# A projection that fills idle TensorE time, in one chain through all stages of a decoder step, and a recurrence prepared per unit five steps ahead

## The reference

```python
h = rmsnorm(x) @ w_in     # fq fk fv ff fz hq hf hi hz mq mz ga gb gm, 1024 -> 8712 columns
o_fox = softmax(q k^T * scale + cq - ck) v            # 8 heads x 64, causal, 2048 rows
S = exp(bl)[..., None] * S + (k * exp(bl - b))^T v    # 4 heads x 128, state 128 x 128
o_mem = softmax(q mk^T * scale) mv                    # 4 heads x 128, 256 tokens
y = x + (sigmoid(ga)*ya + sigmoid(gb)*yb + sigmoid(gm)*ym) @ w_o
```

## Time and profile before

| | us |
|---|---|
| three runs | 3645.16, 3646.96, 3648.72 |
| median | 3646.96 |
| the profiled execution | 3645.66 |
| its span, first to last instruction | 3644.1 |

### The profile page before, as it was taken

One profiled execution on the slowest core, in us unless ns is written; L12 is line 12 of the kernel. 1 busy time (PEld: TensorE's weight loads), 2 busy tenths in 40 slices (PEclk: granted clock), 3 DMA queues, 4 the chain that ended last, 5 costly groups with the idle time before them and its releaser, 6 DMA issues. The chain is left out here.

```text
span 3644.1 us, 38245 instructions
## 1 busy us (share of the span) xinstructions
PE 2951.2 (81%) x13930; PEld 2335.6 (64%) x13930; DVE 1490.2 (41%) x2774; ACT 954.3 (26%) x1806; POOL 581.9 (16%) x539
## 2 busy tenths in 40 slices
PE   4969999999239777868499999999922386799999
PEld 3847777887127565657377787778822232588887
DVE  3510001111345454553455555555556622544444
ACT  1201111111023232222244454444400110423222
POOL 2021111110252324140201002020035300000000
PEclk8979999999559898989799999999966698899999
DMA  3325422211446454534555545554366476533331
GB/s 133 104 63 160 144 67 70 70 67 51 162 152 199 150 169 144 186 121 155 168 151 148 157 130 151 150 157 138 100 211 203 129 220 193 189 114 115 120 120 47
DMA packets 304488, 499.36 MB, mean 137 GB/s; under 512 B 109028, under 2 KB 150535, under 8 KB 285607
## 3 DMA queue, kind: packets, MB, share of 16 engines
q1 hardware_dynamic: 298399, 479.43, 41.9%
q0 software_dynamic: 5904, 17.51, 1.6%
HBM read 386.18 MB, written 110.67 MB: 136 GB/s over the span
## 5 line engine op out<-in xcount | busy, mean ns | idle before, releaser
L2246 PE MATMUL hgfill_out<-hgfill_w_hi,hgfill_x 128*128 128x512 f32 x1024 | 360.4, 429 | 77.4 <-DMA hgfill_x<-x_tiles 50.9
L2246 PE MATMUL fill_out<-fill_w_hi,fill_x 128*128 128x512 f32 x1024 | 374.4, 418 | 0.0
L477 DVE TENSOR_TENSOR in_stage<-in_stage,in_out 128x512 f32<-128x512 f32 x64 | 44.0, 687 | 624.3 <-ACT in_stage L466 624.3
L2246 PEld LDWEIGHTS hgfill_out<-hgfill_w_hi,hgfill_x 128*128 128x128 f32 x1024 | 204.3, 205 | 128.2 <-issue 53.5
L823 DVE TENSOR_TENSOR fox_pt_lo<-fox_turned,fox_pt_hi 128x512 fp32r<-128x512 f32 (+1 forms) x320 | 194.9, 609 | 191.5 <-ACT fox_pt_hi L773 189.9
L773 ACT ACTIVATE fox_pt_hi<-fox_turned 128x512 fp32r<-128x512 f32 (+1 forms) x320 | 170.4, 533 | 361.2 <-PE fox_turned L728 360.6
L809 DVE CUSTOM_DVE_ANT_0 fox_probs<-fox_scores,fox_bias 128x512 f32<-128x512 f32 (+2 forms) x320 | 187.8, 609 | 108.3 <-PE fox_scores L717 66.9
L179 PE MATMUL in_out<-x_hi,in_whi 128*128 128x512 f32 x512 | 205.9, 402 | 19.8 <-POOL in_wlo L421 19.8
L466 ACT ACTIVATE in_stage<-in_out 128x512 f32<-128x512 f32 x112 | 67.0, 599 | 588.0 <-PE in_out L181 588.0
L2246 PE MATMUL hgfill_out<-hgfill_w_lo,hgfill_x 128*128 128x512 f32 x512 | 217.5, 425 | 0.0
L2246 PE MATMUL fill_out<-fill_w_lo,fill_x 128*128 128x512 f32 x512 | 212.2, 414 | 0.0
(11 more groups left out here) (374 smaller groups left out, 6141.4 us busy)
## 6 DMA issues: line engine op xcount, KB each, us to landing
hgfill_x<-x_tiles SPq DMA_DIRECT2D x64, 1024.0 KB, 5.5
fill_x<-x_tiles SPq DMA_DIRECT2D x64, 1024.0 KB, 5.4
paged_slot<-in_cache_fox_k_dram SPq DMA_DIRECT2D x128, 256.0 KB, 3.0
paged_slot<-in_cache_fox_v_dram SPq DMA_DIRECT2D x128, 256.0 KB, 3.0
mf_gate<-plain SPq DMA_DIRECT2D x96, 256.0 KB
turned<-in_stage SPq DMA_DIRECT2D x64, 256.0 KB
plain<-fill_stage SPq DMA_DIRECT2D x64, 256.0 KB, 5.4
in_raw<-in_w_in_dram SPq DMA_DIRECT2D x56, 256.0 KB, 3.1
```

The lines of the kernel that those rows point to most:

```text
L477: dve.tensor_tensor(stage[u % STAGES][:], stage[u % STAGES][:], out[u % STAGES][:], ALU.mult).then_inc(taken, 1)
L2246: ins = pe.matmul(self.out[n % self.OUTS][:], x, w, start=(k == 0 and term == 0), stop=(ends and term == 2))
```

## The change

One Filler with all eight groups lives from the sample stages to the end of `attend_memory`, and each stage says how many of the 3200 matmuls it takes: 40 in `unpack_sample`, 190 in 16 slots of `attend_cache`, 170 in 10 slots of `recur_sample`, 1750 in 138 slots of the recurrence, 120 in 9 slots ahead of the first key step of `attend_prompt`, 80 in its 640 slots, and the 850 left in 66 slots of `attend_memory`. The loops of the sample stages are written out, since slots differ. `lower_bound` moves into `unpack_sample`. To leave two PSUM banks to the Filler, `attend_memory` has one bank of scores and one of turned probabilities where it had two of each. In the recurrence `prepare` comes after `early` and `late` of a step, five steps ahead of the unit's first chunk, five steps with no chunk go first, SP stores a finished piece two steps later and loads a unit three steps earlier. The Filler stores a unit when the next one ends.

```diff
 def recur_prompt(...):
+    PARTS, AHEAD = 4, 5
     def walk(prepare, early, late, post, extra):
-        for n, (blk, h, c) in enumerate(chunks):
-            if n == 0:
-                prepare(0)
-            if c == 0 and n // CH + 1 < len(units):
-                prepare(n // CH + 1)
-            early(n)
-            if n > 0:
+        for n in range(-AHEAD, len(chunks)):
+            if n >= 0:
+                early(n)
+            if n >= 1:
                 late(n - 1)
-            if blk > 0 and n % BLOCK in POST_AT:
-                post(blk - 1, POST_AT.index(n % BLOCK))
+            if n >= BLOCK and n % BLOCK in POST_AT:
+                post(n // BLOCK - 1, POST_AT.index(n % BLOCK))
+            u, at = divmod(n + AHEAD, CH)
+            if at == 0 and u < len(units):
+                for part in range(PARTS):
+                    prepare(u, part)
             extra(n)
...
 def attend_memory(...):
-        scores, turned, o_sum = psum("scores", 2), psum("turned", 2), psum("o_sum", 1)[0]
+        scores, turned, o_sum = (psum(n, 1)[0] for n in ("scores", "turned", "o_sum"))
+        fill.begin(fill.spread(matmuls, 2 * paged.GROUPS + 2))
...
             for u in range(NT + 2):
+                if u == 0:
+                    extra(0)
+                    extra(1)
...
                     elif u < NT:
                         values(n // paged.SLOTS, n % paged.SLOTS)
+                    if u < NT:
+                        extra(2 + u * PER + n % PER)
...
-                        if n >= 2:
-                            pe.wait_ge(exp_ready, n - 1)
+                        if n >= 1:
+                            pe.wait_ge(exp_ready, n)
...
 class Filler:
     def sync(self, sp, slot):
         for n in self.units_ending(self.until(slot), self.until(slot + 1)):
             g = self.group_of(self.first_unit, n)
             m = self.first_x[g] + n - self.first_unit[g]
             if not self.is_sample(n) and m + self.RING < self.first_x[-1]:
                 self.load_x(sp, m + self.RING)
-            self.store(sp, n)
+            if n >= 1:
+                self.store(sp, n - 1)
+            if n == self.units - 1:
+                self.store(sp, n)
...
+MATMULS = {"unpack": 40, "cache": 190, "sample": 170, "recur": 1750, "first": 120, "fox": 80}
```

More of the change, by code:

```diff
@@ L495, in attend_prompt @@
     quads = [(h, q) for h in range(FH) for q in range(QUADS)]
-    steps = [("set", 0)] + [("keys", 0, b) for b in range(QUADS)]
+    steps = [("fill", 0), ("set", 0)]
+    for b in range(QUADS):
+        steps += [("fill", 1 + b), ("keys", 0, b)]
     for i in range(4):
-        steps += [("score", 0, i, 0), ("exp", 0, i)]
+        steps += [("score", 0, i, 0), ("fill", 1 + QUADS + i), ("exp", 0, i)]
+    FILLS = 1 + QUADS + 4
     for n, (h, q) in enumerate(quads):
@@ L653, in _ @@
                     load_bias(0)
-                    fill.sync_start(sp)
                     for n in range(2):
@@ L1493, in _ @@
                 act.activation(sigmoid[:], part[0][:], ACT.Sigmoid).then_inc(sigmoid_ready, 1)
+                act.wait_ge(asked, 1)
+                act.activation(shifted[:], shifted[:], ACT.Exp).then_inc(exp_ready, 1)
+                fill.scalar(act, 0)
+            @block.tensor
+            def _(pe):
+                fill.tensor(pe, 0)
 class CacheAttention:
@@ L1795, in tensor_values, with attend_cache, walk, nothing @@
         m.then_inc(self.slot_free, 1)
-def attend_cache(nc, core, *arguments):
+def attend_cache(nc, core, fill, matmuls, *arguments):
     with ExitStack() as ctx:
         a = CacheAttention(nc, core, ctx, *arguments)
+        fill.begin(fill.spread(matmuls, 2 * a.GROUPS))
+        order = [(it, s) for it in range(a.ROUNDS) for s in range(a.SLOTS)]
+        def walk(keys, middle, values, extra):
+            for n, (it, s) in enumerate(order):
+                keys(it, s)
+                extra(n)
+            middle()
+            for n, (it, s) in enumerate(order):
+                values(it, s)
+                extra(a.GROUPS + n)
+        def nothing(*_):
+            return None
         with nc.Block() as block:
@@ L1885, in _ @@
                     sp.dma_start(primer[i:i + 1, :], core.ident[0:1, :]).then_inc(stored[i], 16)
-                with sp.Fori(0, B // 2) as it:
+                fill.sync(sp, 0)
+                for it in range(B // 2):
                     for i in range(2):
@@ L1912, in _ @@
                 m.then_inc(turned_ready, 1)
+                fill.tensor(pe, 0)
                 pe.wait_ge(step, 2 + 2 * HH)
-                with pe.Fori(0, B // 2) as it:
+                for it in range(B // 2):
                     for i in range(2):
@@ L1925, in _ @@
                 m.then_inc(back_ready, 1)
+                fill.tensor(pe, B + 1)
+            @block.gpsimd
+            def _(pool):
+                for slot in range(fill.slots):
+                    fill.gpsimd(pool, slot)
             @block.vector
@@ L1937, in _ @@
                 link.done[0] += 1
-                with dve.Fori(0, B // 2) as it:
+                for it in range(B // 2):
                     for i in range(2):
@@ L1965, in _ @@
                 act.sem_inc(taken, 2)
-                with act.Fori(0, B // 2) as it:
+                fill.scalar(act, 0)
+                for it in range(B // 2):
                     for i in range(2):
@@ L2203, in matmuls_of, with begin, spread, left @@
         return (len(group.tiles) - 1) * 3 * KT + KT * (5 if group.sample is not None else 3)
+    def begin(self, counts):
+        base = self.edges[-1]
+        self.edges = [base + sum(counts[:n]) for n in range(len(counts) + 1)]
+        self.slots = len(counts)
+        assert self.edges[-1] <= self.total
+    @staticmethod
+    def spread(matmuls, slots):
+        return [matmuls * (n + 1) // slots - matmuls * n // slots for n in range(slots)]
+    def left(self):
+        return self.total - self.edges[-1]
     def until(self, slot):
-        return self.total * min(slot, self.slots) // self.slots
+        return self.edges[slot]
     def group_of(self, counts, n):
```

384 lines of the change are left out of this document (201 added, 183 removed).

## The result

| | before | after |
|---|---|---|
| median us | 3647.24 (4 runs, 3645.16 to 3648.72) | 3860.43 (4 runs, 3850.31 to 3871.83) |
| the profiled execution | 3645.66 | 3871.83 |
| its span | 3644.1 | 3870.0 |

The changed kernel is slower: the ratio is 1.0586, with a 95% interval of 1.0556 to 1.0616. The forecast was 3790, with a range of 3560 to 3920.

What follows compares the result with a forecast made beforehand. PE was taken to bound the forget-gate attention and the memory value half, DVE and POOL the key half; samples +124, recurrence -56, forget-gate -264 and memory +340 gave +144 on 3645.7, 3790 us, range 3560 to 3920.

Steps and rivals of the forecast that it cites:

- Rival 2: Memory attention: the ring of pages doesn't run empty to any cost; stage grows by 130, total 3580; chance 0.17.
- rival 4: Forget-gate attention without fills falls to 1.2 GHz, so no saving there; total about 4050; chance 0.08.
- Rival 3: Middle stages give more: recurrence 583, forget-gate heads 62 each; total 3640 with memory term in full; chance 0.10.
- rival 5: Both stall terms half as big, unit ends 3 us less, samples at lower bound; total 3641; chance 0.10.
- The memory term, +340: Memory attention from 430.2 to about 770 us, as SP waits at 35 unit ends; bounds +200 and +420.
- A value step: Memory attention's value half: from 23.5 to 46.6 us a step, x 8 = 373, plus 25 for lower clock.
- A key step: Memory attention's key half: from 22.0 to 34 us a step by SP's waits, x 8 = 272.
- Samples, +124: Sample stages from 122.6 to about 247 us: unpack_sample +23, attend_cache +49, recur_sample +52; bounds +80 and +165.
- The recurrence, -56: Recurrence from 716.2 to about 660 us, with the 50.9 us of tile waits gone; bounds -140 and -20.
- It stays in one piece, so this wait stays: Recurrence: ACT's 11.5 us unit preparation still makes PE wait 15 times, 3.5 each, 52 against 60.0 us.
- The forget-gate attention, -264: Forget-gate attention with unpack_new from 912.1 to about 648 us: start 58, eight heads of 72, tail 14.
- The two pages named ahead: Skill pages cited for forget-gate turns (transpose mode doesn't engage busy clock) and memory attention (another issuing engine saves only issue time).

Runs made afterwards that it cites:

- e2: Kernel before, with SP waiting after every second group of pages in the memory attention until that group is used up, no Filler there: 3853.0 us.
- e6: Changed kernel with the Filler's tile loads and stores of the memory attention issued by ACT after its copy of a unit: 3690.6 us.
- e8: Changed kernel with ACT issuing the fills' transfers in the memory attention, the memory cache's attention and the samples' recurrence: 3630.0 us.
- e12b: Kernel before with one edit: in the recurrence SP stores the norm's rows two steps later, behind the Filler's loads: 3587.2 us, ratio 0.9843.
- e9: Changed kernel without fills in sample stages and memory attention (old memory attention), SP's stores of the norm's rows back in their own step: 3639.2 us, ratio 0.9983.
- e3: Changed kernel with no fills in the memory attention, its 850 put in the forget-gate attention (930 there), single banks kept: 3670.6 us.

## Why the prediction was right, and where it was off

**The sign and the mechanism held.** The whole is a loss because fills moved out of a stage with cover for many of them into one where each unit's end stops SP. The runs show it from three sides: the wait without the Filler costs 202 us (e2), the Filler without the wait is 168 us cheaper (e6), and the trace has SP's stands where the order put them. Some 17 waits of 5 to 8 us for value pages were forecast; there are 14, 7.9 on average. Rival 2 (pages arrive in time although SP waits) fell by the same rows, rival 4 (the clock of the forget-gate attention) by 0.92 in that stretch, 0.94 from 1867.6 to 2475.0. Rival 3 asked for a recurrence of 583 and heads of 62, rival 5 for samples at +80: they measured 640.5, 74.9 and +156.

**The memory term, +340, measured +385, was made of wrong parts, and that it is only 45 off is partly luck.** The runs give, for a step, before, with single banks, with fills, and with SP's stand:

- A value step: 23.1, 27.4, 42.0 and 56.0, where the forecast had 46.6 and 3.1 for the clock. Its sum starts from 13.9 + 4.6 = 18.5 and leaves out, without a reason, the rests that are in a step now (4.6 by these numbers, 5.0 by its own 23.5). It has the single banks right (4.3 for 4.3), the fills too low (11.7 for 14.6), and SP's stand with the clock about right (15.7 - 4 + 3.1 = 14.8 for 14.0).
- A key step: 24.4, 27.0, 30.5 and 39.5, where the forecast had 34. It starts from an undisturbed step of 22.0 and not from the mean of 24.4, has nothing for single banks (2.6) and nothing for fills (3.5 in the mean, most of it from the first step), and too much for SP's stand (12 for 9.0).

"PE is mostly idle, so fills as such are free" was thus nearly right for the key half, where SP doesn't stand; the terms that failed are the rests left out (59 us over 16 steps) and the fills of the value half. The middle grew by 9, where 11 was forecast: from the last scores of the key half to the first of the value half 61.4 us, 37.4 before, and each holds one key step.

**Samples, +124, measured +156:** `unpack_sample` 27 longer (23 with the 5 of `lower_bound` taken off), the cache 68 against 49, the samples' recurrence 65 against 52. In parts: 65 SP's stand, 71 fills, 18 the start, read as POOL's slices. The stand has its clock here too: a matmul of the memory cache's value pages takes 1014 ns in the median after and 592 in e8. SP's stand was seen; that fills of 0.18 each would be added on top of it, in stages with 87 us of idle PE, was priced at little but in the value groups.

**The recurrence, -56, measured -76.** That the waits for tiles come from SP's stores was right, and was worth more than the rows said: 50.9 us of waits went and 62 us of time with them (e12b), 75.0 came back and 82 with them (e9). Where the few us beyond the waits come from was not traced. The failed step is "It stays in one piece, so this wait stays": the wait for turned keys went from 60.0 to 3.7, but 32.4 came back on ACT's copies of units, which I had not listed; together 36 stand against the 52 of the sum. That the place of the preparation would bring little was right for a wrong reason: it moved the wait.

**The forget-gate attention, -264, measured -249:** read where the forecast read them, at the first turns of probabilities (1786.6 before, 1882.5 after) and the last `fox_pt_lo` (2643.4 and 2481.7), the start is 50 us and not 58, and the eight heads are 599, 74.9 each and not 72. In the midst of them a head takes 77.5 (six from one load of `fox_bias` to the seventh, 1925.95 to 2391.04). The 10 us for engines in step were 13. The estimate rested on 0.228 us for a fill that leaves; the price falls as fills leave (e3), so the last ones gave back only 0.16.

**The two pages named ahead.** The prediction calls the turns of the forget-gate attention ordinary matmuls with an identity. They are not: the kernel makes them with `pe.transpose` (L731), and the built program has these matmuls marked as transposes. The sentence of "TensorE: Matmul & The Clock Gate", Part 4, in the Trainium skill, which is on transpose mode, therefore bears on them directly. From 1867.6 to 2475.0 the trace has 1177 of them among 2945 matmuls, and the granted clock was 0.94. So turns mixed with other matmuls did not hold the clock down here; no run has a stretch of turns alone, and whether the sentence holds for one stays open. As for "Trainium Kernel Development and Optimization", Key Constraints, in the Trainium skill: that another issuing engine saves only issue time did not hold here. The same transfers issued by ACT made the stage 168 us shorter; what they had cost was SP's order, not its issue time. That transfers of all queues share the same engines, as that section says, fits the tile's 6.4 us beside pages and the pages' 3.6 to 4.2 us beside tiles (3.0 without).

**Open:** how much of the 58 us is banks and how much the walk with its slots was not taken apart, nor how much of SP's stand is waiting and how much the lower clock behind it. What of the recurrence's last 14 us belongs to the preparation, to the fills ahead of the first chunk or to 150 more fills is not settled.

## What to carry to other kernels

A queue that issues in order is a resource like an engine: before work is put between two loads, ask what the issuing engine will wait for there, and what else it would have asked for in the meantime. A ring of four gives no cover if its own issuer waits for the last one to be used. The edit that paid (a ratio of 0.984 with a few lines) was to let a store that must wait stand behind loads that need not; to move filling work into "idle" engine time pays only where that engine doesn't set the pace (with SP free, six key steps took their fills for 1.1 us a step, a value step for 14.6), and its price has to be taken at the margin, since it rose from 0.16 to 0.25 us a matmul within one stage.

## What the runs showed of the hardware that was not expected

In the memory stage a tile of 1 MB took 5.5 us (median from issue to landing) when SP issued tiles and pages, and 6.4 when ACT issued the tiles. A page took 3.0 without tiles (e3), and beside them 4.2 in the key half and 3.6 or 3.7 in the value half, whichever engine issued the tiles. So the two streams slow each other, but by little beside the 168 us.

An emptied ring costs more than the wait: after 7.5 us of standing the clock was 0.50, and the next group's matmuls took 6.02 us and not 3.60, although PE waited for no page within them.
